# A decoder step on one core: the order of the operations within an attention slot on TensorE

## The chip, the core and the metric

The kernel runs on one core of one Trainium2 chip. The metric is the device time of one execution in microseconds. Three runs of the kernel before are shown, and their median counts.

## What is computed

The kernel is one inference step of a small decoder: a layer of gated linear attention (GLA), a projection of shared keys and values, and a layer of forgetting attention (FoX), for a prompt of 2048 tokens and for 8 sample tokens with paged caches. The change lies in the attention of the prompt, which is this part of the reference (16 heads of 64 columns, `T` = 2048):

```python
s = jnp.einsum('bqhd,bkhd->bhqk', q_blk, k_all, preferred_element_type=jnp.float32)
s = s + fq_blk.transpose(0, 2, 1)[..., None] - f_k[:, :, None, :]
s = jnp.where((kpos[None, :] <= qpos[:, None])[None, None], s, -jnp.inf)
p = jax.nn.softmax(s, axis=-1)
return jnp.einsum('bhqk,bkhd->bqhd', p.astype(v_all.dtype), v_all)
```

`F` is the running sum of the log-forget values; `f_k` is its value at the key, `fq_blk` at the query. Everything is float32. The kernel gets float32 precision of the logits out of several products of split operands: a high part (`hi`), a low part (`lo`) and a third pair of tiles (`more`) that holds the forget sums and the row maxima.

## The kernel before, in words

`attention_phase` (line 1531) writes one program for each engine. The work is cut into 8 **steps**; a step handles a pair of heads, of which one stands in each half of the array (`two_heads`, line 1808). A step has 41 **slots**, numbered by `e` from 0 to 40. The engines go through the same slots in the same order, each at its own pace, and wait for each other by semaphores. `run_steps` (line 1676) writes the first and the last step out, and the six between them as a loop of three turns with two steps in each.

Slots 0 to 39 each handle one **unit** `(G, i)`: query group `G` of 512 queries against key tile `i` of 128 keys. Group 0 has slots 0 to 3, group 1 slots 4 to 11, group 2 slots 12 to 23, group 3 slots 24 to 39. The last four units of a group lie on the diagonal; they are 512, 384, 256 and 128 queries wide. On TensorE (function `unit`) a slot has these parts:

- `logits_wait`: waits, above all for the exponential of two slots before, which frees the bank pair for the logits.
- `masks` (line 1805, `hide_kq`), in units on the diagonal: two small matmuls write the mask into the logits' bank pair.
- `logits` (line 1811, out of `kT` and `qT`, written `psum<-at_qT_..,at_kT_..` in the profile since the moving operand stands first): four pairs of matmuls. ScalarE then takes the exponential (`exponential`, line 1977) into one of five tiles `at_p`, and GpSimd adds it to a running sum (`add`, lines 2142 to 2149).
- `maxima` (line 1811, `psum<-at_kT_hi,at_qT_hi`): one pair of matmuls for another part of the score matrix, up to 512 columns wide. VectorE subtracts the forget sums and takes the row maxima of them (lines 2022 to 2024), which the logits of a later slot need. There is one bank pair for them (`bank_max`), so `max_wait` (line 1827) waits until VectorE is through with the maxima of the slot before. Slots 0 to 15 do the maxima of the step's own last query group, slots 16 to 39 those of the next step's first three.
- Where the maxima lie on the diagonal (slots 12 to 19, 21, 23, 25, 27, 30, 33, 36 and 39), a mask goes into `bank_max` first (`hide_qk`), and `max_wait` stands ahead of that mask.
- `weigh_v` (line 1891): the product of the exponentials of the slot before with the values, one pair of matmuls into `bank_o`.
- `turn_op`: in some slots one **turning operation** in `bank_turn`. It is a transpose of rows of q or k (`turn`, line 1820, in slots 9, 11, 13, 18, 21, 25, 32, 35), of the maxima (`m_row`, line 1838, slots 17, 23, 30, 40), or a step of the softmax's denominator (`sums`, `pick_sums`, `spread_out`, lines 1845, 1852, 1859, in slots 2 to 4, 6 to 8, 14 to 16, 26 to 28).

What the other engines do for a turning operation stands in their own slot, behind the slot's main work: ScalarE makes the high part of a `turn` (line 1968) behind the slot's exponential, and VectorE the low part (line 2013), `at_share`, `at_spread` and `at_o` (lines 2057, 2059, 2067), behind the slot's maxima. VectorE also multiplies and sums the pages of the sample caches, behind the rest of the slot (lines 2048 and 2051, in slots 1, 10, 20, 33 and 5, 12, 29, 38). SyncE issues the loads and stores of a slot. The table `turn_slots` and the list `max_slots` say which slot has what.

Of the kernel before, what the change touches and what calls it, by code (L numbers as in the profile page):

```python
# [1530 lines left out]
def attention_phase(nc, g):  # L1531
# [4 lines left out]
    UN = len(exp_units)  # L1536
# [50 lines left out]
    with ExitStack() as st:  # L1587
# [50 lines left out]
        def following(j, u):  # L1638

            return (j, 1) if u == 0 else (j + 1, 0)  # L1640

        def previous(j, u):

            return (j, 0) if u == 1 else (j - 1, 1)

        def whose(who, j, u):

            return following(j, u) if who == NEXT else previous(j, u) if who == LAST else (j, u)
# [4 lines left out]
        def slots_of(j, u):  # L1653

            return start_slots if is_first(j, u) else end_slots if is_last(j, u) else mid_slots

        def before(j, u):

            return FIRST if is_first(j, u) else FIRST + AT_START - EACH + EACH * (2 * j + u)
# [34 lines left out]
        with nc.Block() as block:  # L1694
# [106 lines left out]
            def _(pe):  # L1801
                def masks(bank_at, col, hide):

                    for a in range(2):
                        pe.matmul(bank(bank_at + a)[:, col:col + P], g.ident16[:, :], hide[:, :], start=True, stop=False,
                                  skip_group_check=True)

                def two_heads(bank_at, cols, left, right, l_cols, r_cols, first, last):

                    for a in range(2):  # L1810
                        mm = pe.matmul(bank(bank_at + a)[:, cols], left[half[a], l_cols], right[half[a], r_cols],  # L1811
                                       start=first, stop=last, skip_group_check=True)
                    return mm

                def turn(j, u, base, a, b, n, at=bank_turn, spare=0):
                    if (a, b) == (0, 0):
                        pe.wait_ge(rows_loaded, 32 * (2 * j + u) + 32)
                    pe.wait_ge(turn_used, base + n + 1 - spare)
                    for r in range(R):
                        mm = pe.transpose(at[:, r * P:(r + 1) * P], rows[b][:, R * a + r, :], g.ident[:, :])  # L1820
                    mm.then_inc(turn_full, 1)

                def max_wait(j, u, t, c, n, spare=0):
                    h = 2 * j + u
                    if t % R == 0 and c == 0:
                        pe.wait_ge(turn_hi, 2 * NG * h + 2 * (t // R) + 2)
                    pe.wait_ge(max_done, UN * h + n + 1 - spare)

                def maxima(j, u, t, c, at=bank_max):
                    w = min(NB, (t + 1) * P - c * NB)  # L1830
                    keys, diagonal = slice(c * NB, c * NB + w), c == t // R
                    two_heads(at, slice(0, w), hi[0][u], hi[1][u], slice(t * P, (t + 1) * P), keys, not diagonal, True)\
                        .then_inc(max_full, 1)

                def m_row(j, u, base, G, n, at=bank_turn, spare=0):
                    pe.wait_ge(m_ready, NG * (2 * j + u) + G + 1 + 1)
                    pe.wait_ge(turn_used, base + n + 1 - spare)
                    pe.matmul(at[0:2 * R, 0:P], m[:, :], g.ident[:, :], start=True, stop=True).then_inc(turn_full, 1)

                def sums(j, u, base, G, n):  # L1840
                    pe.wait_ge(p_added, UN * (2 * j + u) + units_to(G) + PT)
                    pe.wait_ge(turn_used, base + n + 1)
                    for b in range(4):
                        strip, half_ = slice(P // 4 * b, P // 4 * (b + 1)), slice(b // 2 * NB // 2, (b // 2 + 1) * NB // 2)
                        mm = pe.matmul(bank_turn[strip, 0:NB // 2], ones[:, :], p_sum[G % 2][:, b % 2, half_], start=True, stop=True)
                    mm.then_inc(turn_full, 1)

                def pick_sums(j, u, base, G, n):
                    pe.wait_ge(turn_used, base + n + 1)
                    columns = bank_turn[:, 0:2 * R].rearrange("p (h r a) -> p h r a", h=2, r=2)  # L1850
                    for r in range(2):
                        mm = pe.matmul(columns[:, :, r, :], sum_rows[:, r * P:(r + 1) * P],
                                       pick[:, :].rearrange("p (h a) -> p h a", h=2), start=True, stop=True)
                    mm.then_inc(turn_full, 1)

                def spread_out(j, u, base, G, n):
                    pe.wait_ge(spread_ready, NG * (2 * j + u) + G + 1)
                    for r in range(R):
                        mm = pe.transpose(bank_turn[:, r * P:(r + 1) * P], spread[:, r * P:(r + 1) * P], g.ident[:, :])
                    mm.then_inc(turn_full, 1)  # L1860

                def logits_wait(j, u, e):
                    h = 2 * j + u
                    G, i = exp_units[e]
                    if e == 0:
                        pe.wait_ge(f_loaded, 32 * h + 32)
                    if i == 0:
                        pe.wait_ge(m_stored, 64 * (NG * h + G) + 64 + 64)
                    pe.wait_ge(p_ready, UN * h + e + 1)

                def logits(j, u, e):
                    G, i = exp_units[e]
                    skip = max(0, i - R * G) * P
                    keys, queries, cols = slice(i * P, (i + 1) * P), slice(G * NB + skip, (G + 1) * NB), slice(skip, NB)
                    b = bank_st[e % 2]
                    two_heads(b, cols, hi[1][u], hi[0][u], keys, queries, i < R * G, False)
                    two_heads(b, cols, hi[1][u], lo[0][u], keys, queries, False, False)
                    two_heads(b, cols, lo[1][u], hi[0][u], keys, queries, False, False)
                    two_heads(b, cols, more[1][u], more[0][u], keys, queries, False, True).then_inc(st_full, 1)
# [15 lines left out]
                def turn_op(j, u, base, kind, a, b, n):  # L1895
                    if kind == "turn":
                        turn(j, u, base, a, b, n)
                    if kind == "m_row":
                        m_row(j, u, base, a, n)
                    if kind == "sum":  # L1900
                        sums(j, u, base, a, n)
                    if kind == "pick":
                        pick_sums(j, u, base, a, n)
                    if kind == "spread":
                        spread_out(j, u, base, a, n)

                def unit(j, u, e):

                    slot = slots_of(j, u)[e]
                    maxes = [(whose(who, j, u), t, c, n) for who, kind, t, c, n in slot if kind == "max"]  # L1910
                    if e < UN:
                        G, i = exp_units[e]
                        logits_wait(j, u, e)
                        if i >= R * G:
                            masks(bank_st[e % 2], (i - R * G) * P, g.hide_kq)
                    for at, t, c, n in maxes:
                        if c == t // R:
                            max_wait(*at, t, c, n)
                            masks(bank_max, t % R * P, g.hide_qk)
                    if e < UN:  # L1920
                        logits(j, u, e)
                    for at, t, c, n in maxes:
                        if c != t // R:
                            max_wait(*at, t, c, n)
                        maxima(*at, t, c)
                    if e:
                        weigh_v(j, u, e - 1)
                    for who, kind, a, b, n in slot:
                        turn_op(*whose(who, j, u), before(j, u), kind, a, b, n)

                def step(j, u):
                    for e in range(UN + 1):
                        unit(j, u, e)
# [701 lines left out]
```

## Time and profile before

| | |
|---|---|
| median of three runs | 3391.19 us (3386.99 to 3394.28) |
| the profiled execution's own time | 3391.84 us |
| its span in the profile | 3390.2 us |
| TensorE busy | 3059.6 us (90%) |
| VectorE, ScalarE, GpSimd busy | 1577.1, 1005.0, 753.8 us |
| mean granted clock of TensorE | 0.92 of full speed |
| the attention of the prompt | from about 2186 to 3128 us of the span |

Busy time is the time in which an engine had an instruction under way. Of a matmul the profile models the end, and the matmuls of a stream overlap, so the length of a piece of TensorE's work is read from the start of its first matmul to the start of what follows. An idle time in brackets behind a row is the time in which the engine stood still before that row, and names whom it waited for. The granted clock is 1.00 at 2.4 GHz and 0.50 at 1.2 GHz. The profiled execution lies 0.65 us above the median of the three runs.

### The profile page before, as it was taken

The numbers are of one execution on the slowest core, as the hardware profiler recorded it, in microseconds if no ns is written. First come the engines' busy times: TensorE is split into PE (matmuls) and PEld (weight loads), VectorE is DVE, ScalarE is ACT, GpSimd is POOL, SyncE is SP. The second block draws the span as 40 slices with busy tenths as digits, with TensorE's granted clock in tenths as the row PEclk, the third lists the DMA queues.
The fourth block names the chain that finished last, engine by engine and source line by source line (L and its number), as shares of the span: only waits on it lengthen the run. The fifth ranks groups of instructions, "written<-read, shape, count | busy, mean of one in ns | idle before, by whom it ended". The sixth has DMA issues, their size and how long they took to land. (4 is left out here: it accounts for less than half of the span.)

```text
span 3390.2 us, 44717 instructions
## 1 busy us (share of the span) xinstructions
PE 3059.6 (90%) x16468; PEld 2207.9 (65%) x16468; DVE 1577.1 (47%) x3597; ACT 1005.0 (30%) x1596; POOL 753.8 (22%) x430
## 2 busy tenths in 40 slices
PE   6599999997799959999969999789999999998799
PEld 2378887886678848888968888544444444443567
DVE  1622122212777637421146411377676767772433
ACT  0411222212555643200352211033433333433100
POOL 1300000000000002000020000247666766777000
PEclk8698999998899979999769998689999999998899
DMA  9421122212566542121041120333133213301874
GB/s 342 160 76 72 47 80 77 75 47 106 166 215 194 161 142 93 72 72 48 20 154 56 63 75 38 89 101 86 40 101 99 85 42 93 104 30 38 272 233 128
DMA packets 265388, 355.11 MB, mean 105 GB/s; under 512 B 23917, under 2 KB 156013, under 8 KB 265090
## 3 DMA queue, kind: packets, MB, share of 16 engines
q1 hardware_dynamic: 262820, 344.10, 30.7%
q0 software_dynamic: 2304, 8.39, 0.7%
q8 instruction: 120, 1.97, 0.2%
q14 instruction: 72, 0.58, 0.1%
q10 hardware_dynamic: 72, 0.07, 0.0%
HBM read 250.15 MB, written 102.10 MB: 104 GB/s over the span
## 5 line engine op out<-in xcount | busy, mean ns | idle before, releaser
L2149 POOL TENSOR_TENSOR at_p_sum<-at_p_sum,at_p 128x1024 f32<-128x1024 f32 (+3 forms) x264 | 541.8, 2052 | 107.7 <-ACT at_p L1977 97.2
L1977 ACT ACTIVATE at_p<-psum 128x1024 f32<-128x1024 f32 (+1 forms) x320 | 286.7, 896 | 468.6 <-PE psum L1811 465.5
L2024 DVE CUSTOM_DVE_ANT_0 psum<-psum,at_f_wide 128x512 f32<-128x512 f32 (+3 forms) x640 | 376.7, 630 | 0.8 <-issue 0.8
L1891 PE MATMUL psum<-at_p,at_v 128*64 128x512 f32 (+3 forms) x1280 | 304.5, 556 | 0.1
L564 PE MATMUL psum<-kv_w_hi,kv_h_hi 128*128 128x512 f32 (+1 forms) x640 | 245.0, 383 | 17.4 <-DVE kv_h_lo L474 17.4
L565 PE MATMUL psum<-kv_w_lo,kv_h_hi 128*128 128x512 f32 (+1 forms) x640 | 245.0, 383 | 0.0
L566 PE MATMUL psum<-kv_w_hi,kv_h_lo 128*128 128x512 f32 (+1 forms) x640 | 244.8, 383 | 0.0
L892 POOL TENSOR_TENSOR kv_hs_lo<-kv_stage,kv_hs_hi 128x64 fp32r<-128x64 f32 x1 | 0.3, 318 | 1078.7 <-ACT kv_hs_hi L648 1078.7
L564 PE MATMUL psum<-gla_w_hi,gla_h_hi 128*128 128x512 f32 x512 | 201.4, 393 | 0.0
L565 PE MATMUL psum<-gla_w_lo,gla_h_hi 128*128 128x512 f32 x512 | 200.2, 391 | 0.0
L566 PE MATMUL psum<-gla_w_hi,gla_h_lo 128*128 128x512 f32 x512 | 200.1, 391 | 0.0
L564 PEld LDWEIGHTS psum<-kv_w_hi,kv_h_hi 128*128 128x128 f32 x640 | 137.4, 215 | 37.6 <-issue 17.4
L1811 PE MATMUL psum<-at_qT_hi,at_kT_hi 64*128 64x512 f32 (+3 forms) x640 | 151.8, 471 | 0.0
L566 PEld LDWEIGHTS psum<-kv_w_hi,kv_h_lo 128*128 128x128 f32 x640 | 137.6, 215 | 20.1
L565 PEld LDWEIGHTS psum<-kv_w_lo,kv_h_hi 128*128 128x128 f32 x640 | 137.6, 215 | 20.2
L1811 PE MATMUL psum<-at_kT_hi,at_qT_hi 64*128 64x512 f32 (+3 forms) x640 | 129.0, 400 | 13.9 <-DVE at_chunk_max L2024 13.7
L2022 DVE COPY at_max_seen<-one 128x1 f32<-128x1 f32 x320 | 48.4, 151 | 187.9 <-PE psum L1811 184.7
L2323 PE MATMUL psum<-out_w_hi,out_og_hi 128*128 128x512 f32 x272 | 108.5, 399 | 27.8 <-DVE out_og_lo L2417 27.8
L1891 PEld LDWEIGHTS psum<-at_p,at_v 128*64 128x64 f32 x1280 | 64.3, 135 | 96.0 <-issue 89.2
L786 DVE COPY gla_stage<-psum 128x512 f32<-128x512 f32 x48 | 33.2, 691 | 193.9 <-PE psum L566 193.9
L1811 PE MATMUL psum<-at_qT_lo,at_kT_hi 64*128 64x512 f32 (+3 forms) x640 | 119.5, 369 | 0.0
L1811 PE MATMUL psum<-at_q_more,at_k_more 64*128 64x512 f32 (+3 forms) x640 | 119.0, 368 | 0.0
(437 smaller groups left out, 6568.1 us busy)
## 6 DMA issues: line engine op xcount, KB each, us to landing
mod_w<-in_ada_w SPq DMA_DIRECT2D x12, 2048.0 KB, 18.1
at_f_wide<-F SPq DMA_DIRECT2D x32, 512.0 KB, 5.2
at_page<-in_cache_k SPq DMA_DIRECT2D x32, 512.0 KB, 3.6
gla_w_raw<-in_gla_w_in SPq DMA_DIRECT2D x6, 2048.0 KB, 8.7
mod_w<-in_kv_ada_w SPq DMA_DIRECT2D x4, 2048.0 KB, 9.8
v_gla<-gla_stage SPq DMA_DIRECT2D x32, 256.0 KB, 2.0
sg_gla<-gla_stage SPq DMA_DIRECT2D x32, 256.0 KB, 2.0
gl_sg<-sg_gla SPq DMA_DIRECT2D x16, 512.0 KB
```

The lines of the kernel that those rows point to most:

```text
L564: pe.matmul(out, left[0], right[0], start=first, stop=False)
L565: pe.matmul(out, left[0], right[1], start=False, stop=False)
L566: return pe.matmul(out, left[1], right[0], start=False, stop=last)
L786: dve.tensor_copy(out, ps).then_inc(evac_done, 1)
L892: pool.tensor_tensor(hs_lo[:, :, 0:NS], f_tile[0][:, 0:K * NS].rearrange("p (k c) -> p k c", c=NS), hs_hi[:, :, 0:NS].bitcast(F32), ALU.su ...
L1811: mm = pe.matmul(bank(bank_at + a)[:, cols], left[half[a], l_cols], right[half[a], r_cols], start=first, stop=last, skip_group_check=True)
L1891: mm = pe.matmul(bank_o[half[a], skip:NB], v[u][:, i, half[a]], p_tile[e % PT][:, a, skip:NB], start=(i == 0), stop=(i == R * G + R - 1), ...
L1977: act.activation(p_tile[e % PT][:, :, skip:NB], pair_of(bank_st[e % 2])[:, :, skip:NB], ACT.Exp)\
L2022: dve.tensor_copy(max_seen[:, n:n + 1], g.one[:, :])
L2024: op = dve.tensor_tensor_reduce(pair_of(at(n))[:, a, 0:w], pair_of(at(n))[:, a, 0:w], f_wide[:, a, c * NB:c * NB + w], 1.0, -3.0e38, ALU.s ...
L2149: pool.tensor_tensor(p_sum[s][:, :, skip:NB], p_sum[s][:, :, skip:NB], p_tile[e % PT][:, :, skip:NB], ALU.add).then_inc(p_added, 1)
L2323: pe.matmul(ps_y[u][a][:, :], left[0], w_hi[:, k, cols], start=(k == 0), stop=False)
```

## The change

Within a slot on TensorE the parts get another order. The order was masks, logits, maxima, value product, turning operation. It becomes masks, maxima, logits, turning operation, value product. Nothing else is changed: the same instructions with the same operands, banks and waits, and the programs of the other four engines are the same, row for row.

```diff
                         if c == t // R:
                             max_wait(*at, t, c, n)
                             masks(bank_max, t % R * P, g.hide_qk)
-                    if e < UN:
-                        logits(j, u, e)
                     for at, t, c, n in maxes:
                         if c != t // R:
                             max_wait(*at, t, c, n)
                         maxima(*at, t, c)
+                    if e < UN:
+                        logits(j, u, e)
+                    for who, kind, a, b, n in slot:
+                        turn_op(*whose(who, j, u), before(j, u), kind, a, b, n)
                     if e:
                         weigh_v(j, u, e - 1)
-                    for who, kind, a, b, n in slot:
-                        turn_op(*whose(who, j, u), before(j, u), kind, a, b, n)
```

The first place is TensorE from the maxima of slot 24 to those of slot 25, in the first step of the loop's body. `at_kT_hi0,at_qT_hi0` are maxima, `at_p3,at_v1` is the value product of slot 23, `hide_qk` the mask for the maxima of slot 25, and the four rows of `at_qT..1` and `at_q_more1` are logits. The rows before:

```order
L1811 MATMUL psum<-at_kT_hi0,at_qT_hi0 128x512 x2
L1891 MATMUL psum<-at_p3,at_v1 64x128 x2
L1827 REGISTER_ALU
L1805 MATMUL psum<-hide_qk,ident16 128x128 x2
L1811 MATMUL psum<-at_qT_hi1,at_kT_hi1 128x512 x2
L1811 MATMUL psum<-at_qT_lo1,at_kT_hi1 128x512 x2
L1811 MATMUL psum<-at_qT_hi1,at_kT_lo1 128x512 x2
L1811 MATMUL psum<-at_q_more1,at_k_more1 128x512 x2
L1811 MATMUL psum<-at_kT_hi0,at_qT_hi0 128x384 x2
```

Behind the maxima stood the value product and then the mask, which waits for VectorE; the logits of slot 25 came after that wait. The rows of the change:

```order
L1811 MATMUL psum<-at_kT_hi0,at_qT_hi0 128x512 x2
L1811 MATMUL psum<-at_qT_hi1,at_kT_hi1 128x512 x2
L1811 MATMUL psum<-at_qT_lo1,at_kT_hi1 128x512 x2
L1811 MATMUL psum<-at_qT_hi1,at_kT_lo1 128x512 x2
L1811 MATMUL psum<-at_q_more1,at_k_more1 128x512 x2
L1891 MATMUL psum<-at_p3,at_v1 64x128 x2
L1827 REGISTER_ALU
L1805 MATMUL psum<-hide_qk,ident16 128x128 x2
L1811 MATMUL psum<-at_kT_hi0,at_qT_hi0 128x384 x2
```

The logits of slot 24 now stand between its maxima and the waiting mask, and the maxima of slot 25 follow their mask directly.

The second place is TensorE from the maxima of slot 11 to the mask of slot 12, in the same step; slot 11 has a turning operation (`at_k_rows`), and its logits are 128 queries wide. The rows before:

```order
L1811 MATMUL psum<-at_kT_hi1,at_qT_hi1 128x512 x2
L1888 REGISTER_ALU
L1891 MATMUL psum<-at_p0,at_v1 64x256 x2
L1818 REGISTER_ALU
L1820 MATMUL psum<-ident,at_k_rows 128x128 x4
L1868 ISA
L1827 REGISTER_ALU
L1805 MATMUL psum<-hide_qk,ident16 128x128 x2
```

The value product (`at_p0,at_v1`) came first, then the turning operation. The rows of the change:

```order
L1811 MATMUL psum<-at_kT_hi1,at_qT_hi1 128x512 x2
L1811 MATMUL psum<-at_qT_hi1,at_kT_hi1 128x128 x2
L1811 MATMUL psum<-at_qT_lo1,at_kT_hi1 128x128 x2
L1811 MATMUL psum<-at_qT_hi1,at_kT_lo1 128x128 x2
L1811 MATMUL psum<-at_q_more1,at_k_more1 128x128 x2
L1818 REGISTER_ALU
L1820 MATMUL psum<-ident,at_k_rows 128x128 x4
L1888 REGISTER_ALU
L1891 MATMUL psum<-at_p0,at_v1 64x256 x2
L1868 ISA
L1827 REGISTER_ALU
L1805 MATMUL psum<-hide_qk,ident16 128x128 x2
```

The logits of slot 11 moved in behind its maxima, and the turning operation moved ahead of the value product.

## Rows read from the trace of the kernel before

**Rows 1.** Windows: us; PE, PEld, DVE, ACT, POOL busy; granted clock, DMA, GB/s.

```profile
2452.57:2563.55 110.98, 103.71 (x729) 52.88 (x730) 80.01 (x240) 44.22 (x56) 76.95 (x37) 1.00 0.28 82
...
3018.00:3115.00 97.00, 92.50 (x618) 43.98 (x620) 44.00 (x108) 38.91 (x48) 72.87 (x34) 0.98 0.08 28
```

**Rows 2.** Waits of PE in the step from 2452.57: total, times, longest.

```profile
PE psum L1805 <- DVE at_chunk_max L2024: 4.7, 7, 1.2
PE psum L1838 <- DVE at_m L2030: 2.1, 2, 1.1
PE psum L1811 <- DVE at_chunk_max L2024: 1.5, 3, 0.8
```

**Rows 3.** Timeline of PE, slots 24 and 25: start, duration, then instruction.

```profile
2519.86 0.39 PE L1811 MATMUL psum<-at_kT_hi,at_qT_hi 64*128 64x512 f32 x2
2520.18 0.44 PE L1891 MATMUL psum<-at_p,at_v 128*64 128x128 f32 x4
2521.82 0.29 PE L1805 MATMUL psum<-hide_qk,ident 128*128 128x128 bf16 x2 [1.20 <-DVE at_chunk_max L2024]
2522.03 0.50 PE L1811 MATMUL psum<-at_qT_hi,at_kT_hi 64*128 64x512 f32 x2
...
2523.07 0.33 PE L1811 MATMUL psum<-at_kT_hi,at_qT_hi 64*128 64x384 f32 x2
2523.33 1.08 PE L1891 MATMUL psum<-at_p,at_v 128*64 128x512 f32 x4
2524.34 0.66 PE L1820 MATMUL psum<-ident,at_k_rows 128*128 128x128 f32 x4
```

**Rows 4.** Timeline of DVE, the maximum of slot 24, first and last instruction.

```profile
2520.29 0.15 DVE L2022 COPY at_max_seen<-one 128x1 f32<-128x1 f32 x1 [0.67 <-PE psum L1811]
...
2521.62 0.14 DVE L2024 DVE_READ_ACCUMULATOR2_ANT at_chunk_max<- 128x1 f32 x1
```

**Rows 5.** Timeline of PE, narrow pieces: slot 22, then slot 23.

```profile
2514.20 0.39 PE L1811 MATMUL psum<-at_qT_hi,at_kT_hi 64*128 64x256 f32 x2
...
2514.77 0.48 PE L1811 MATMUL psum<-at_kT_hi,at_qT_hi 64*128 64x512 f32 x2
2515.18 0.87 PE L1891 MATMUL psum<-at_p,at_v 128*64 128x384 f32 x4
...
2517.17 0.33 PE L1811 MATMUL psum<-at_qT_hi,at_kT_hi 64*128 64x128 f32 x2
...
2517.67 0.33 PE L1811 MATMUL psum<-at_kT_hi,at_qT_hi 64*128 64x256 f32 x2
```

**Rows 6.** Timeline of PE, value product of slot 11 and masks of slot 12.

```profile
2483.07 0.65 PE L1891 MATMUL psum<-at_p,at_v 128*64 128x256 f32 x4
...
2485.22 0.29 PE L1805 MATMUL psum<-hide_qk,ident 128*128 128x128 bf16 x2 [0.92 <-DVE at_chunk_max L2024]
```

**Rows 7.** Timeline of DVE, page products of slots 10 and 20.

```profile
2482.44 1.35 DVE L2048 TENSOR_TENSOR at_page<-at_page,at_q_sample 128x1024 f32<-128x1024 f32 x1
...
2511.12 3.00 DVE L2048 TENSOR_TENSOR at_page<-at_page,at_q_sample 128x1024 f32<-128x1024 f32 x1
```

**Rows 8.** Timeline of POOL, the sums beside these two products.

```profile
2481.43 1.28 POOL L2149 TENSOR_TENSOR at_p_sum<-at_p_sum,at_p 128x512 f32<-128x512 f32 x1 [0.57 <-ACT at_p L1977]
...
2510.67 2.36 POOL L2149 TENSOR_TENSOR at_p_sum<-at_p_sum,at_p 128x1024 f32<-128x1024 f32 x1 [0.22 <-ACT at_p L1977]
```

**Rows 9.** Timeline of ACT: the exponential and the turning copy of slot 25.

```profile
2523.27 1.02 ACT L1977 ACTIVATE at_p<-psum 128x1024 f32<-128x1024 f32 x1 [1.69 <-PE psum L1811]
2525.03 0.60 ACT L1968 ACTIVATE at_kT_hi<-psum 128x512 fp32r<-128x512 f32 x1 [0.74 <-PE psum L1820]
```

**Rows 10.** Timeline of DVE, what follows that copy.

```profile
2525.66 0.69 DVE L2013 TENSOR_TENSOR at_kT_lo<-psum,at_kT_hi 128x512 fp32r<-128x512 f32 x1 [1.02 <-ACT at_kT_hi L1968]
```

**Rows 11.** Timeline of PE, masks of slot 12 in the last step.

```profile
3050.80 0.27 PE L1805 MATMUL psum<-hide_qk,ident 128*128 128x128 bf16 x2 [1.76 <-DVE at_chunk_max L2024]
```

**Rows 12.** Window of two microseconds behind that gap; PEclk is the granted clock.

```profile
3054.00:3056.00 2.00, 2.00 (x12) 1.27 (x10) 0.29 (x3) 0.45 (x1) 0.00 (x0) 0.50 0.43 94
```

## Prediction

> **What bounds the kernel now.** I read the windows first, one per step. In a middle step of 110.98 us TensorE (PE) is busy 103.71 us, VectorE (DVE) 80.01, GpSimd (POOL) 76.95 and ScalarE (ACT) 44.22 [rows 1]. So PE bounds the attention, and all that an order of its instructions can win is its idle time: 7.3 us of a step, and 55 over seven such steps and a last one with 4.5. Whatever precedes and follows the attention is untouched and is shifted one to one.
>
> The list of PE's waits says where the 7.3 us are [rows 2]: 4.7 in seven waits of the masks for the maxima (L1805), 1.5 in three waits of the other maxima (L1811), and 1.05 in one wait of the row of maxima (L1838; the list counts two, as the window begins and ends with one). All of them end with VectorE. The seven mask waits lie in slots 12, 13, 21, 23, 25, 30 and 39, the three others in slots 1, 3 and 11.
>
> The timelines say why. From the start of the maxima of slot 24 the next masks start 1.96 us later [rows 3]: DVE starts 0.43 us after the pair (0.53 where the pair is the first of its kind and takes 0.50), works 1.47 us [rows 4], and 0.06 us pass until the masks. In that time PE has only the value product, then stands still for 1.20. The logits, 1.04 us of work that waits for nothing here, are queued behind the waiting mask.
>
> **The change, part by part.** It adds and removes no instruction. PE's lengths from start to start are [rows 3, 5]: logits 1.04, 0.57 and 0.50 us for 512, 256 and 128 columns; maxima 0.32 in front of a value product; value product 1.01, and by the same 0.07 less than the row's duration 0.80, 0.58 and 0.37 for the narrower ones; masks 0.21; a turning transpose 0.59. Of pairs of one kind the first costs 0.1 more, whichever it is, and so does the change from pairs of 64 rows to the others at the end. I take the moved work as neutral. Bounds: 0.03 us either way in each of 320 slots, a third of that first-pair cost, thus 10 us either way.
>
> The waits do change. Between two maxima PE now always has logits, turning operation and value product; before, the logits were missing where masks wait. DVE needs 0.53 + 1.47 + 0.06 = 2.06 us from the maxima to their release. A full slot gives 0.32 + 1.04 + 1.01 = 2.37, one with a turning operation more. So a wait is left only where the slot is short or DVE has other work. Per step:
> - **Slots 13, 21 and 30** fall to nothing. Of the seven mask waits slot 25 has 1.20 [rows 3] and slot 12 has 0.92 [rows 6], so the other five share 2.6; into these three full logits of 1.04 are put.
> - **Slots 11, 23 and 39**: the slot ahead has logits 256 and a value product 384 wide (in slot 38, 256 and 384 too): 0.34 + 0.57 + 0.80 + 0.21 for the next logits' mask = 1.92, against 2.06: 0.15 each, 0.45 together.
> - **Slot 25**: 0.32 + 1.04 + 0.37 = 1.73, against 2.06: 0.34 instead of 1.20.
> - **Slot 1**: slot 0 has no value product: 0.34 + 1.04 + 0.21 = 1.59: 0.5, as now.
> - **Slot 3**: between nothing and the 0.8 that is the longest of its kind [rows 2]. I take 0.3.
> - **Slot 40**, the row of maxima: it follows the maxima of slot 39, with DVE's page sum of slot 38 in between. The logits of slot 39 move into that time and the value product of slot 39 moves out: 1.2 instead of 1.05.
> - **Slot 12** is the dear one. It follows slot 11, and the page product stands on DVE between the maxima of slots 10 and 11. Now it took 1.35 us, because POOL's sum had 0.27 us left when it began [rows 7, 8]. In slot 20 POOL's sum began 0.45 us ahead of the product and lasted 2.36, and the product took 3.00 [rows 7, 8]: it waits for the end of the sum and then runs. In the new order both shift. The maxima of slot 10 start first, and DVE is ready for the product 2.0 us later. The logits end at about 1.0 (0.34 + 0.57 and the tail of the last pair). The exponential covers 512 elements and so takes 0.60, as the copy of 512 does [rows 9], and POOL begins its sum of 1.28 [rows 8] at 1.7, ahead of DVE. The product then runs from 3.0 to 4.1, the maxima of slot 11 on DVE to 5.6. PE passes the maxima of slot 11 at 2.06 and needs 0.9 for them with the logits, 0.59 for the turning operation and 0.58 for the value product [rows 3, 5, 6]; it is at the masks of slot 12 at 4.1 and waits 1.5 to 1.6, instead of 0.92 [rows 6].
>
> The Trainium skill (page "SBUF — State Buffer", section "SBUF: two separate sides") says that VectorE and GpSimd share a pair of ports which goes to the instruction that starts first, for its whole length, and that a VectorE operation with two inputs in SBUF counts there. By it slot 12 costs the 1.6 that I take from slot 20; by the 1.35 that the same product shows now it would cost 0.55, and the kernel would be 7 us faster than my number.
>
> Sum per step: 0.45 + 0.34 + 0.5 + 0.3 + 1.2 + 1.6 = 4.4 instead of 7.3, thus 2.9 less. There are seven such steps: 20 us. The last step has no maxima for a next one, only 4.5 us of idle time (97.00 less 92.50 in its window [rows 1]), and waits most at slot 12; I take 1 us. Together 21 us: 3391.84 - 21 = 3370.8 for the profiled execution, which lies 0.65 above the median; so 3370 us.
>
> What I cost at nothing, with its cover: the value product comes later in its slot by a turning operation. ACT's copy of the finished group waits for it (0.59 us at slots 4, 12, 24), and the next value product into that bank follows a full slot of 2.37 later; the exponential of 1.02 and the copy of 0.60 [rows 9] fit into that with some 0.5 us to spare. If that cover were gone, the price would be three short waits per step. ACT now finds the exponential ahead of the turning copy: the copy takes 0.60 [rows 9] and starts up to 1 us after the transpose instead of 0.03 after it, and DVE's low part (0.69) [rows 10] ends later in front of the next maxima. I find this late part beside or at most 0.5 us behind the maxima's arrival, which the slots behind the transposes still hold. SyncE's queue keeps its order; it waits for maxima and turning operations that come no later than before.
>
> **The rivals.** First, **the waits come back**: the maxima have one bank pair, DVE is busy 80 of 111 us, and what PE no longer waits in one slot it waits in the next. For it: waits in slots 12 and 13 and in 21, 23, 25 follow closely. Against it: rows 3 show a full 1.04 us of work behind the wait, and a full slot leaves 0.3 us. If all come back the time stays at 3391.
>
> Second, **slower**: the late low part decides. If DVE is through with it later than I reckon by y, PE waits behind each of the eight transposes; their slots hold 0.1 to 0.8 us, 3.1 together. A step then loses 8y - 3.1. The gain of 2.9 is gone at y = 0.75, and the point at which it reads as slower is about y = 0.9. For a y of 1.02, one whole exponential more ahead of the copy [rows 9], seven steps lose 7 x 5.1 = 35 us: 3391 + 35 - 21 = 3405. For it: eight transposes in every step, two engines in a row behind them, all strictly in their slots' order. Against it: ACT is busy only 44 of 111 us, and one exponential ahead is already in my reckoning.
>
> Third, **the clock falls behind the long gap of slot 12**. In the last step PE waited 1.76 us there [rows 11], and from 3054 to 3056 us the granted clock was 0.50 [rows 12], the lower level of 1.2 GHz. PE was busy for all of these 2 us, so the fall cost 1 us there, and I take 1.3 with its edges. In the middle step, with a longest gap of 1.2, the clock was 1.00 throughout [rows 1]. My gap of 1.6 lies near the bad one, though without the second wait that followed there. If it falls in seven steps: 9 us, 3379. The Trainium skill (page "TensorE: Matmul & The Clock Gate", section "A second HAM failure mode: psum-queue depth-cycling") says that frequent short idles between groups of matmuls can make the clock swing; the 1.00 of the middle step speaks against that here.
>
> Fourth, the page product of slot 10 comes ahead of POOL after all: slot 12 costs 0.55, seven steps 7 us less, 3363.
>
> **How the numbers follow.** A measurement of this kernel tells about 0.2%, 7 us, from no change. The forecast with slot 12 at 1.6 and a steady clock: 0.36. Clock rival: 0.16. The product ahead of POOL, or a still larger gain: 0.18. Waits come back, wholly or nearly: 0.17. Late low part: 0.13. The first three are faster, with 0.70; some of the small gains fall to no change either way, which I count within the 0.17. Range: the low end is 3363 less 9 for the bound of the moved work, 3354; the high end takes in 3379 and the returning waits up to 3391, so 3392. Slower by more lies outside, with little of the rest.
>
> **What would show it.** Right: per step the mask waits fall from 4.7 to about 2.2, with 1.6 of it at slot 12 and none at 13, 21 and 30; slot 25 near 0.34; the page product of slot 10 near 2.1; a middle step of about 108 us; PE busy still near 103.7. Wrong: waits of L1811 that grow by what L1805 loses; DVE idle for ACT's copies ahead of maxima that are already full; a granted clock of 0.50 behind slot 12; or PE's busy time of a step off by more than 1 us, which would mean that the moved matmuls have another price.

## The result and the profile after

The changed kernel takes 3368.27 us (median of 4 runs, 3363.85 to 3371.95) against 3390.72 (4 runs, 3386.99 to 3394.28) for the kernel before in the same measurement: a ratio of 0.9933, with an interval of 0.9916 to 0.9951. The forecast was 3370 in a range of 3354 to 3392. The profiled execution took 3369.64 us, with a span of 3367.8.

The windows of the profile after come first: a middle step, from one row of maxima (L1838) to the next, and the last step, both as in [rows 1].

```profile
2450.03:2557.19 107.16, 103.65 (x729) 52.36 (x730) 75.60 (x240) 43.25 (x56) 76.74 (x37) 1.00 0.29 85
...
3004.88:3101.88 97.00, 92.82 (x624) 44.35 (x624) 39.61 (x105) 39.76 (x49) 74.31 (x35) 0.98 0.08 27
```

The step is 3.8 us shorter, from 110.98 to 107.16. PE's busy time in it is the same (103.71 before, 103.65 now), so all of it is idle time: 7.27 us before, 3.51 now. VectorE is also busy for 4.4 us less, with the same 240 instructions: 3.9 of it in the four copies of L2059 and 0.7 in the page products (L2048). That I had not forecast, and the experiments take it up. PE's waits in the same step, to be held against [rows 2]:

```profile
PE psum L1838 <- DVE at_m L2030: 2.1, 2, 1.0
PE psum L1805 <- DVE at_chunk_max L2024: 1.7, 2, 1.4
PE psum L1811 <- DVE at_chunk_max L2024: 0.5, 1, 0.5
```

Of the seven mask waits (L1805) two are left, at slots 12 and 25, with 1.7 us instead of 4.7; of the three waits of other maxima (L1811) the one of slot 1 is left. The row of maxima at slot 40 is unchanged (the view again counts it at both ends). How a slot looks now is seen in PE's timeline of slots 24 and 25, the place of [rows 3]:

```profile
2514.68 0.50 PE L1811 MATMUL psum<-at_kT_hi,at_qT_hi 64*128 64x512 f32 x2
2515.02 0.40 PE L1811 MATMUL psum<-at_qT_hi,at_kT_hi 64*128 64x512 f32 x2
...
2516.04 0.44 PE L1891 MATMUL psum<-at_p,at_v 128*64 128x128 f32 x4
2516.75 0.28 PE L1805 MATMUL psum<-hide_qk,ident 128*128 128x128 bf16 x2 [0.27 <-DVE at_chunk_max L2024]
2516.96 0.44 PE L1811 MATMUL psum<-at_kT_hi,at_qT_hi 64*128 64x384 f32 x2
```

From the start of the maxima to the next masks it is 2.07 us, against 1.96 before. VectorE's part of the round is what it was; the 0.1 more is that of a pair which is the first of its kind (0.50 against 0.39). But 1.0 us of logits now stands in that time, so PE is idle for 0.27 of it and not for 1.20.

**The sum over the kernel.** From the row of maxima at the start of the first step to the first matmul of the output phase (L2352) it was 903.45 us and is 884.99: 18.5 less. A second profile of the changed kernel (the run x8_changed_again below) gives 883.70. The rest of the 22 us lies in phases that the change does not touch and that differ between two executions of one kernel: ahead of that row the profile after is 3.7 us longer (2228.21 against 2224.55), and behind L2352 it was 262.2 us before, 254.6 and 261.7 in the two profiles after. So some 4 of the 22 us are not shown to come from the change. Step by step the gain is 3.84, 2.36, 3.82, 1.69, 3.91, -0.96 and 2.54 us, and 1.26 in the last one: uneven, although the steps do the same work. The fourth and the sixth begin with the jump back of the loop; in the second and the seventh the clock fell (both below).

### The profile page after: what moved, and what is told of

It is laid out like the page before. It is cut to its first block and busy times, and to the rows that moved or that the text cites. A ratio compares the mean times of both kernels' runs of the same rounds, so it can differ in the third digit from the quotient of the medians.

```text
span 3367.8 us, 44729 instructions
## 1 busy us (share of the span) xinstructions
PE 3060.4 (91%) x16468; PEld 2206.5 (66%) x16468; DVE 1543.5 (46%) x3597; ACT 998.0 (30%) x1596; POOL 751.5 (22%) x430
## 5 line engine op out<-in xcount | busy, mean ns | idle before, releaser
L1811 PE MATMUL psum<-at_kT_hi,at_qT_hi 64*128 64x512 f32 (+3 forms) x640 | 157.1, 489 | 9.9 <-DVE at_chunk_max L2024 8.9
L1811 PEld LDWEIGHTS psum<-at_kT_hi,at_qT_hi 64*128 64x128 f32 x640 | 63.0, 194 | 100.9 <-DVE at_chunk_max L2024 49.6
L1811 PE MATMUL psum<-at_qT_hi,at_kT_hi 64*128 64x512 f32 (+3 forms) x640 | 121.9, 377 | 0.0
L1811 PE MATMUL psum<-at_qT_lo,at_kT_hi 64*128 64x512 f32 (+3 forms) x640 | 119.6, 370 | 0.0
L1811 PE MATMUL psum<-at_qT_hi,at_kT_lo 64*128 64x512 f32 (+3 forms) x640 | 119.3, 368 | 0.0
```

## The experiments

I had two theories. By the first (theory A), the logits behind the maxima carry the gain, and the turning operation ahead of the value product is worth little; by the rival (theory B) the gain comes from the turning operation's new place, which gives VectorE the low part of a transpose earlier. The first two runs each do one half.

**x1_max_first**: only the logits move behind the maxima.

```diff
-                    if e < UN:
-                        logits(j, u, e)
                     for at, t, c, n in maxes:
                         ...
                         maxima(*at, t, c)
+                    if e < UN:
+                        logits(j, u, e)
                     if e:
                         weigh_v(j, u, e - 1)
```

> The change's first half alone: slots run as masks, maxima, logits, value product, turning operation. Theory A (the gain comes from putting the logits between two maxima; moving the turning operation ahead of the value product adds little): most of the gain stays, 3369 to 3376 us against 3391 before and 3368 with the whole change. The mask waits of a middle step fall from 4.7 us to 2 to 3, and 0.3 to 0.6 us come back at slots 10 and 22, where VectorE's low part of a transpose now ends 0.5 us behind the arrival of the maxima. Theory B (the gain comes from giving VectorE its low part earlier, by the turning operation's new place): little of the gain stays, 3384 us or more, and the mask waits stay above 4 us a step.

Measured: 3380.51 us (5 runs, 3376.03 to 3388.70) against 3394.75, a ratio of 0.9955 [0.9941, 0.9968]. This half gains 14 us or so, two thirds of the whole. Theory B wanted 3384 us or more; theory A's range of 3369 to 3376 is missed on the slow side by 4.5 us. The waits that come back in a middle step are not at slots 10 and 22, as expected, but for the maxima of slots 9, 11 and 29 (0.55, 0.76 and 0.72 us).

**x2_turn_first**: only the turning operation moves ahead of the value product.

```diff
-                    if e:
-                        weigh_v(j, u, e - 1)
                     for who, kind, a, b, n in slot:
                         turn_op(*whose(who, j, u), before(j, u), kind, a, b, n)
+                    if e:
+                        weigh_v(j, u, e - 1)
```

> The change's second half alone: masks, logits, maxima, turning operation, value product. Theory A: no gain, 3386 to 3394 us, and the seven mask waits of a middle step stay near 4.7 us, since the logits still stand behind the masks' wait. Theory B: at least half of the gain, 3380 us or less.

Measured: 3418.62 us (5 runs, 3412.41 to 3419.36), ratio 1.0068 [1.0055, 1.0082]. It is slower by 24 us, which neither theory had expected. The halves do not add: 0.9955 and 1.0068 together would give a kernel slower than before, and the whole change has 0.9933. The windows of a middle step of x1_max_first, then of x2_turn_first, show it in PE's idle time, 5.39 and 9.43 us (before 7.27, with the whole change 3.51):

```profile
2680.28:2788.77 108.49, 103.10 (x728) 52.54 (x729) 78.00 (x240) 44.26 (x57) 76.37 (x37) 1.00 0.30 84
```

```profile
2694.79:2808.92 114.13, 104.70 (x729) 52.38 (x729) 79.42 (x240) 43.37 (x56) 76.95 (x37) 1.00 0.27 80
```

PE's waits in the step of x2_turn_first name a line that stood nowhere before:

```profile
PE psum L1805 <- DVE at_chunk_max L2024: 4.8, 7, 1.2
PE psum L1838 <- DVE at_m L2030: 2.5, 2, 1.3
PE psum L1859 <- DVE at_spread L2059: 2.1, 3, 0.8
PE psum L1811 <- DVE at_chunk_max L2024: 1.3, 2, 0.8
```

L1859 is a turning operation as well. It spreads the shares of a finished group and waits for VectorE's copy `at_spread` (L2059). PE's timeline of x2_turn_first around one of them, then VectorE's copy, then GpSimd's sum beside it:

```profile
2738.39 0.40 PE L1811 MATMUL psum<-at_kT_hi,at_qT_hi 64*128 64x512 f32 x2
2738.71 0.61 PE L1852 MATMUL psum<-at_pick,at_sum_rows 128*128 128x4 f32 x4
...
2742.49 0.66 PE L1859 MATMUL psum<-ident,at_spread 128*128 128x128 f32 x4 [0.67 <-DVE at_spread L2059]
...
2740.67 1.76 DVE L2059 COPY at_spread<-at_share 128x512 f32<-128x512 f32 x1
...
2739.77 2.37 POOL L2149 TENSOR_TENSOR at_p_sum<-at_p_sum,at_p 128x1024 f32<-128x1024 f32 x1 [0.72 <-ACT at_p L1977]
```

GpSimd's sum began 0.90 us ahead of the copy and ran to 2742.14; the copy ended 0.29 later, at 2742.43, and PE started 0.06 behind it. With the turning operation ahead of the value product, PE comes to L1859 sooner and has nothing left to do there. The length of this copy in the whole program is read from the view of line L2059 (least, median and greatest, in ns), here of the kernel before, of the change, of x1_max_first and of x2_turn_first:

```profile
L2059 DVE COPY at_spread<-at_share x32: 426/1763/2078, 2251.4 to 3122.5; 128x512 f32<-128x512 f32 x32
```

```profile
L2059 DVE COPY at_spread<-at_share x32: 426/426/709, 2253.8 to 3107.7; 128x512 f32<-128x512 f32 x32
```

```profile
L2059 DVE COPY at_spread<-at_share x32: 426/2052/2065, 2256.7 to 3116.8; 128x512 f32<-128x512 f32 x32
```

```profile
L2059 DVE COPY at_spread<-at_share x32: 426/1764/2051, 2253.8 to 3149.6; 128x512 f32<-128x512 f32 x32
```

Each half alone leaves the median copy at 1.76 to 2.05 us; both together let it run in 0.43, and in 0.71 at most. In the kernel before, the 8 copies that start between two sums of GpSimd take 0.43, and each of the 24 that start inside a sum ends 0.28 to 0.29 us behind the sum's end. VectorE's timeline of the change shows one such copy, and GpSimd's the sums around it:

```profile
2493.01 0.43 DVE L2059 COPY at_spread<-at_share 128x512 f32<-128x512 f32 x1
...
2490.12 2.38 POOL L2149 TENSOR_TENSOR at_p_sum<-at_p_sum,at_p 128x1024 f32<-128x1024 f32 x1 [0.71 <-ACT at_p L1977]
2493.28 2.39 POOL L2149 TENSOR_TENSOR at_p_sum<-at_p_sum,at_p 128x1024 f32<-128x1024 f32 x1 [0.77 <-ACT at_p L1977]
```

The copy falls into the 0.78 us between two sums: one ended at 2492.50, the next begins at 2493.28, 0.27 behind the copy's start. The copy itself was not edited; what changed is when the two instructions start. Whether it decides what each half is worth was tested next.

**x5_turn_first_psum, x6_max_first_psum, x10_before_psum**: the two halves and the kernel before, with the reciprocal written to PSUM and the spreading copy read from there. The same edit in all three:

```diff
-                    dve.reciprocal(share[s][:, :], bank_turn[:, 0:2 * R])
+                    dve.reciprocal(bank_turn[:, 2 * R:4 * R], bank_turn[:, 0:2 * R])
...
-                                    share[s][:, :].unsqueeze(2).broadcast_to([P, 2 * R, HD])
+                                    bank_turn[:, 2 * R:4 * R].unsqueeze(2).broadcast_to([P, 2 * R, HD])
```

> The second half alone again (masks, logits, maxima, turning operation, value product), with one more edit: the reciprocal of the sums goes into bank_turn instead of a tile in SBUF, and the copy that spreads it reads it there. The second half alone came out at 1.0068 of before; its trace shows three new waits of 2.1 us in a step, TensorE at the spreading transpose for VectorE's spread, and that copy takes 1.76 to 2.05 us instead of 0.43. Theory F (the copy is held by GpSimd's running sum, and a copy that reads PSUM is not): the copies take 0.4 to 0.8 us whatever GpSimd does, the three waits vanish, and the time falls by 8 x 2.1 = 15 us or more, to 0.9985 to 1.0035 of before. Rival G (the copy is late because the sums are late): the copies or the waits stay and the ratio is above 1.005.

> The first half alone (masks, maxima, logits, value product, turning operation) with the same edit. There the copies took 2.05 us, and TensorE waits 0.55 and 0.72 us for maxima in the slots behind two of them. Theory F: those two waits go, a middle step falls from 108.5 to 107.2 us, and the ratio from 0.9955 to 0.993 (0.9915 to 0.9945), that of the whole change: then what the second half adds to the first is that this copy escapes the sum. Rival H (the second half adds by the earlier low part of the transposes): the ratio stays at 0.9945 or above.

> The kernel before with only the edit of the spreading copy (reciprocal and copy through bank_turn). In the trace of before three copies of a step take 1.76 us, but no wait of TensorE follows them. If the copy matters only where an order leaves no room behind it, nothing is gained: 0.997 to 1.002 of before, mask waits still 4.7 us a step. If the copy was a price of its own before, and the change won by setting it free: 0.995 or less.

In all three the copy took 0.69 us throughout, whatever GpSimd did; the view of L2059 of x6_max_first_psum:

```profile
L2059 DVE COPY at_spread<-psum x32: 690/691/694, 2253.1 to 3098.1; 128x512 f32<-128x512 f32 x32
```

The Trainium skill (page "SBUF — State Buffer", section "Who interferes with whom") says that a VectorE instruction with at most one input in SBUF, outside the modes that use both ports, does not contend with GpSimd. The 0.69 agrees.

PE's waits in a middle step of x5_turn_first_psum, to be held against those of x2_turn_first:

```profile
PE psum L1805 <- DVE at_chunk_max L2024: 4.8, 7, 1.2
PE psum L1838 <- DVE at_m L2030: 2.5, 2, 1.3
PE psum L1811 <- DVE at_chunk_max L2024: 1.3, 2, 0.8
```

The line of L1859 is gone and the others are the same. In x6_max_first_psum the waits of x1_max_first at slots 9 and 29 are gone; the 0.76 at slot 11 is still there.

| kernel | us | ratio to before | the same without the edit |
|---|---|---|---|
| x5_turn_first_psum | 3400.55 (11 runs) | 1.0019 [1.0010, 1.0028] | 1.0068 |
| x6_max_first_psum | 3364.93 (5 runs) | 0.9914 [0.9900, 0.9928] | 0.9955 |
| x10_before_psum | 3394.67 (12 runs) | 0.9994 [0.9985, 1.0004] | 1 |

A short copy is worth nothing in the order before, and 0.4 to 0.5% (14 to 17 us) in either half. So the slowness of x2_turn_first is for the most part the held copy, and theory F stands. In the profiled step of x5_turn_first_psum PE's idle time is back at 7.36 us; what is left of the slowness is busy time, 106.02 us against 103.71 before and 104.70 in x2_turn_first; here the clock also fell in that step (0.98 granted). And x6_max_first_psum, which leaves the turning operation where it was, is as good as the whole change or slightly better (0.9914 against 0.9933 and, repeated, 0.9924).

That the turning operation ahead of the value product is then no gain in itself is seen in PE's busy time, here in the middle step of x6_max_first_psum:

```profile
2668.59:2775.40 106.81, 102.71 (x729) 52.60 (x730) 74.30 (x240) 44.24 (x57) 76.32 (x37) 1.00 0.29 86
```

PE is busy for 102.71 us in it, and for 103.10 in x1_max_first; with the turning operation ahead it is 103.65 (the change) and 104.70 (x2_turn_first, against 103.71 before). That is 0.5 to 1.0 us per step for the same matmuls; a part of it is not the order's price, since x1_max_first and x6_max_first_psum have the same program on PE and differ by 0.4. The timelines show where 0.6 of the 0.9 us between x6_max_first_psum and the change lies. PE at the transpose of slot 9 in x6_max_first_psum, then in the change:

```profile
2694.11 0.66 PE L1820 MATMUL psum<-ident,at_q_rows 128*128 128x128 f32 x4
2694.60 0.28 PE L1805 MATMUL psum<-hide_kq,ident 128*128 128x128 bf16 x2
...
2475.06 0.66 PE L1820 MATMUL psum<-ident,at_q_rows 128*128 128x128 f32 x4
2475.65 1.08 PE L1891 MATMUL psum<-at_p,at_v 128*64 128x512 f32 x4
```

From its start to what follows a transpose takes 0.49 us ahead of a mask that need not wait, and 0.59 ahead of a value product. In the change all twelve transposes of a step (L1820 and L1859) stand ahead of a value product; together they take 7.03 us, against 6.40 in x6_max_first_psum. Why the next instruction matters was not tested.

**x3_page_moved**: the wait that the forecast put highest, slot 12, taken away. The page product of slot 10 goes to slot 6, where no short slot follows.

```diff
-page_at = (1, 5, 10, 12, 20, 29, 33, 38)
+page_at = (1, 5, 6, 12, 20, 29, 33, 38)
```

> The changed kernel, with VectorE's page product of slot 10 moved to slot 6 (page_at), and nothing else. If the 1.44 us that TensorE still waits at slot 12 come from that product, held up by GpSimd's sum, as I reckoned: the wait falls to 0.2 us or less, a middle step from 107.2 to about 105.8 us, and the time by 8 x 1.3 = 10 us, to 3358 (3353 to 3363). Rival (the wait is the shortness of slot 11 itself, 128 columns of logits, whatever VectorE does): the wait stays above 1 us and the time within 3365 to 3371.

Measured: 3352.07 us (4 runs, 3347.94 to 3356.63), ratio 0.9881 [0.9866, 0.9896]. Its step:

```profile
2660.09:2765.73 105.64, 103.56 (x729) 52.27 (x730) 75.68 (x240) 43.25 (x56) 77.25 (x37) 1.00 0.28 86
```

```profile
PE psum L1838 <- DVE at_m L2030: 2.1, 2, 1.0
PE psum L1811 <- DVE at_chunk_max L2024: 0.5, 1, 0.5
PE psum L1805 <- DVE at_chunk_max L2024: 0.3, 1, 0.3
```

The 1.44 us of slot 12 are gone from the masks' line (L1805), and the step is 1.5 shorter. So the page product is what this slot waits for. Eight times 1.5 is 12 us; the change and this kernel differ by 0.52%, 17 us or so, within what the intervals leave, and the time lies 1 us below the expected range. In this profile the stalls at the loop's two jumps, of which the next run tells, were also shorter: 4.0 and 3.7 us, against 4.4 and 8.3.

**x4_unrolled**: the steps that hold the loop's jump gained least. Here the loop is written out.

```diff
-            with eng.Fori(0, PAIRS // 2 - 1) as j:
+            for j in range(PAIRS // 2 - 1):
```

> The changed kernel with the loop over the six middle steps of the attention written out, for all engines. In the changed kernel's trace TensorE stands still for 4.16 and 0.25 us, then 5.57 and 2.72 us, at the two places where the loop jumps back, and the granted clock falls behind them; the trace puts the first of each to a DMA of the row of maxima, the second to issue. Theory C (the jump back is the cause): all of them are gone, steps 4 and 6 take 107 to 108 us instead of 114.1 and 118.0, and the time falls by 10 to 18 us, to 3350 to 3358. Rival D (the DMA of the maxima is late, as the trace names it): the stalls stay and the time is 3364 to 3372. Rival E (a longer program costs as much in instruction loads elsewhere): the stalls are gone, but the time stays at 3364 to 3372.

Measured: 3356.84 us (4 runs, 3354.70 to 3357.70), ratio 0.9891 [0.9876, 0.9906]: 14 us less than the change, within the range of theory C. The rows it answers are PE's first masks behind the jumps in the kernel before, two of them, and in the change, four:

```profile
2567.63 0.39 PE L1805 MATMUL psum<-hide_kq,ident 128*128 128x128 bf16 x2 [3.70 <-DMA at_q_more<-at_m_lo]
...
2794.16 0.39 PE L1805 MATMUL psum<-hide_kq,ident 128*128 128x128 bf16 x2 [3.23 <-DMA at_q_more<-at_m_lo]
```

```profile
2562.09 0.39 PE L1805 MATMUL psum<-hide_kq,ident 128*128 128x128 bf16 x2 [4.16 <-DMA at_q_more<-at_m_lo]
2565.17 0.39 PE L1805 MATMUL psum<-hide_kq,ident 128*128 128x128 bf16 x2 [0.25 <-issue]
...
2784.69 0.39 PE L1805 MATMUL psum<-hide_kq,ident 128*128 128x128 bf16 x2 [5.57 <-DMA at_q_more<-at_m_lo]
...
2790.23 0.39 PE L1805 MATMUL psum<-hide_kq,ident 128*128 128x128 bf16 x2 [2.72 <-issue]
```

The stall was 3.2 to 3.7 us, and is 4.2 and 5.6 in the change, with a second one of up to 2.72 behind which nothing is named but the engine's own issue. In the repeat it is 5.21 + 2.17 and 3.69 + 0.42. Written out, these stalls are gone, and the six steps take 107.2 to 107.6 us, but for one of 108.7 in which the clock fell. So they belong to the jump, not to the transfer that the rows name: SyncE issues the four transfers of that row 1.0 to 3.4 us behind the row of maxima with and without the jump. The kernel before was not run with its loop written out, so how much of the change's gain the jumps take is not measured. The second stall shows in the orders that have the maxima ahead of the logits (0.17 to 2.72 us in eight of ten jumps of five such profiles, one of the eight put down to ScalarE), and not in the kernel before, x2_turn_first, x5_turn_first_psum or x10_before_psum, which have the logits first. What makes it stays open.

**x7_page_unrolled** joins both edits, the moved page product and the written-out loop, to the change; **x9_all** does the same on x6_max_first_psum; **x8_changed_again** is the change once more, beside x5, x6 and x7.

> The changed kernel with both edits that were faster alone: the page product at slot 6 instead of slot 10, and the loop over the steps written out. They touch different waits, so they should add: 0.9891 of before less 8 x 1.5 = 12 us, 0.9855 (0.984 to 0.987). If the page product's gain of 16 us was partly a quieter loop start, less: 0.9875 or above.

> All that was faster, put together: masks, maxima, logits, value product, turning operation (the first half), the spreading copy out of PSUM, the page product at slot 6, and the loop written out. Against the changed kernel with page product and loop (0.9842 of before) a step has some 0.9 us less of TensorE's busy time (102.7 instead of 103.6) and 0.3 us less at the row of maxima, but 0.8 us more of waits at slots 23 and 25: 0.9840 of before (0.982 to 0.986).

> The changed kernel itself, a second time, for what changes from run to run. Expected: the ratio within 0.9915 to 0.9951; steps without a jump back at 107 to 109 us; the stalls at the two jumps back between 3 and 8 us each, not the same as the first time; the stretch behind the attention, 270.6 us before and 262.9 us with the change, anywhere between these, since the change does not reach it. If that stretch is near 263 again, the change does reach it.

| kernel | us | ratio to before |
|---|---|---|
| x7_page_unrolled | 3339.43 (5 runs) | 0.9842 [0.9828, 0.9856] |
| x9_all | 3348.22 (4 runs) | 0.9861 [0.9844, 0.9878] |
| x8_changed_again | 3370.64 (5 runs) | 0.9924 [0.9909, 0.9938] |

The change repeats, with a middle step of 107.12 us. The stretch behind the attention is 261.7 us in it, between the 254.6 of the first profile and the 262.2 before, so nothing shows that the change reaches it. x7_page_unrolled, with steps of 105.9 us, lies in its range: the two gains add. It is the fastest kernel here: 54 us less than before, of which the change is 23 to 26. x9_all misses its range by a little on the slow side. In the order of x6_max_first_psum slot 12 waits for only 0.75 us, so moving the page product can give no more than that there; in x9_all this wait is gone, the 0.77 of slot 11 and the 0.77 of slot 23 are not, and a step is 106.58 us instead of 106.81.

## Why the prediction was right, point by point

- **PE bounds the attention, its idle time is the gain, and the moved work is neutral.** Right: 103.71 us busy before and 103.65 after. That rests partly on two things that cancel, which is luck: the logits behind the maxima lower PE's busy time by 0.6 (x1_max_first), and the turning operation raises it again by as much.
- **Slots 13, 21 and 30 fall to nothing.** Right; none of them waits.
- **Slots 11, 23 and 39, 0.15 each.** No row marks a wait there. From the logits' mask to the maxima of slot 11, and to the masks of slots 23 and 39, it is 0.36 to 0.37 us, some 0.15 beyond the mask's 0.21, as forecast; gaps so small go into the difference between the idle 3.51 and the waits shown.
- **Slot 25, 0.34; slot 1, 0.5; slot 40, 1.2.** Measured 0.27, 0.48 and 1.04. **Slot 3, 0.3**: none.
- **Slot 12, 1.5 to 1.6.** Measured 1.44, by the mechanism named. GpSimd's sum, VectorE's page product, then PE's last pair of slot 11 and the masks of slot 12 (the places of [rows 8], [rows 7] and [rows 6]):

```profile
2478.65 1.27 POOL L2149 TENSOR_TENSOR at_p_sum<-at_p_sum,at_p 128x512 f32<-128x512 f32 x1 [0.68 <-ACT at_p L1977]
...
2478.75 2.26 DVE L2048 TENSOR_TENSOR at_page<-at_page,at_q_sample 128x1024 f32<-128x1024 f32 x1
...
2480.35 0.65 PE L1891 MATMUL psum<-at_p,at_v 128*64 128x256 f32 x4
...
2482.44 0.29 PE L1805 MATMUL psum<-hide_qk,ident 128*128 128x128 bf16 x2 [1.44 <-DVE at_chunk_max L2024]
```

  The sum begins 0.10 us ahead of the product, where the forecast had 0.3; so the order of the two was right by a small margin, though it was the same in all seven steps. The product takes 2.26 us where 2.1 was forecast; before it took 1.35. The 0.55 by the old duration, the fourth rival, did not come. x3_page_moved shows that the page product is the cause.
- **A step of 108, a gain of 2.9.** Measured 107.16 and 3.8: the step is better than the sum. The waits I summed come to 4.4 us, and PE is idle for 3.51; the difference is above all slots 3, 12 and 40 and the small terms.
- **What was not in the sum: the spreading copy.** I moved the turning operation ahead of the value product and checked its transposes and ACT's copy, but not that L1859, a turning operation too, would meet VectorE's copy there. At the copy's length before, an estimate from x2_turn_first is 2.1 us per step, most of the gain. It came out well because the same change shifts the copy in front of GpSimd's sum, which nothing in the prediction foresaw: luck. The cover that I gave is also misplaced in part: of slots 4, 12 and 24 only slot 4 has a turning operation, so at the other two the value product does not come later.
- **What was not in the sum on the other side: the jumps.** I took seven steps as equal, though two of them begin with the jump and took 115.8 and 117.1 us already before. They gained 1.69 and lost 0.96 us where a quiet one gained 3.8, and two others gained 1.3 to 1.5 less than that by the clock. The larger gain of quiet steps does not quite make up for it: the seven steps gained 17.2 us where 20 was forecast, and the last 1.26 where I took 1. That the total of 21 is so near to the 22 measured is luck in part, since the attention gave 18.5 in the profiles.
- **Rival 1, the waits come back**: refuted; L1811 waits for 0.5 us and not 1.5.
- **Rival 2, the late low part**: its premise holds and its price does not. VectorE stands idle for up to 1.5 us until ACT's copy is there, as in this row of VectorE's timeline:

```profile
2487.38 0.69 DVE L2013 TENSOR_TENSOR at_qT_lo<-psum,at_qT_hi 128x512 fp32r<-128x512 f32 x1 [1.54 <-ACT at_qT_hi L1968]
```

  But PE has no wait behind it: the logits, moved into that time, cover it.
- **Rival 3, the clock behind slot 12**: it came in one middle step of seven. In all seven slot 12 waits for 1.43 to 1.45 us. In the step shown at the top the granted clock stayed at 1.00 behind it; in the step before, it fell. PE's row there and the windows from it:

```profile
2373.87 0.28 PE L1805 MATMUL psum<-hide_qk,ident 128*128 128x128 bf16 x2 [1.44 <-DVE at_chunk_max L2024]
```

```profile
2373.00:2375.00 2.00, 1.13 (x10) 0.89 (x12) 1.90 (x11) 0.00 (x0) 0.02 (x1) 0.90 0.00 0
2375.00:2377.00 2.00, 2.00 (x14) 0.82 (x11) 1.20 (x3) 1.01 (x2) 0.00 (x0) 0.50 0.60 150
...
2896.00:2898.00 2.00, 1.59 (x10) 0.86 (x12) 0.80 (x5) 0.54 (x1) 0.09 (x1) 0.71 0.72 256
2898.00:2900.00 2.00, 2.00 (x10) 1.08 (x8) 1.48 (x5) 0.06 (x1) 0.00 (x0) 0.50 0.01 2
```

  The granted clock goes to 0.50, the lower level of 1.2 GHz. The last two rows are a place that I had not named: the start of another step, behind the row of maxima that waited for 1.04 us (at 2896.41). At the start of the steps from 2450.03, 2671.25 and 3004.87 the same wait leaves the clock at 1.00. These two steps gained 2.36 and 2.54 us, 1.3 to 1.5 less than the quiet ones, which is the price of 1.3 that the rival had for one fall. In the repeat, x8_changed_again, the clock also fell behind slot 12 in one step of seven, at another place (2600.93). In the last step the clock falls as before [rows 11, 12], behind 2.08 us.

## What to carry to other kernels

On an engine that works in order, put work that needs nothing ahead of the instruction that waits, and sum what is left slot by slot from the durations of the rows: here seven of eleven waits per step went. Follow every kind of instruction that a moved call can issue, the rare ones too, to the engine it waits for: by x5_turn_first_psum, the one that I forgot accounts for 17 of the 24 us that its move cost when it was made alone. And do not judge the halves of a reordering by themselves: when the length of one engine's instruction hangs on another engine's, what counts is which of the two starts first, and that can shift with any edit.

## What the runs showed of the hardware that I had not expected

- The same VectorE copy of 128 x 512 f32 from SBUF to SBUF took 0.43 us when it started between two GpSimd sums and up to 2.08 when it started behind the begin of one, ending 0.3 behind the sum; read from PSUM it took 0.69, whether a sum ran or not.
- The loop's jump back stalls PE for 3.2 and 3.7 us in the kernel before, and for 4.4 and 8.3 in the change (7.4 and 4.1 in its repeat). With the six steps written out the changed kernel is 0.42% faster (0.9891 against 0.9933).
- The granted clock fell to 0.50 behind one wait of 1.44 us and one of 1.04, while the same waits in other steps left it at 1.00. So the length of the last wait alone does not say whether it falls; what does was not tested.
